# Hybrid decoder trunk: where two retention score stages and two halves of a hidden layer stand in the attention units

## The chip, the cores and the metric

The kernel runs on one core of a Trainium2 chip. The time is that of one execution on the device, in microseconds; the kernel before has a median of 1283.83 us over 3 runs (1283.48 to 1285.69).

## What is computed

Two layers over 256 tokens of width 1024, all in float32. Each layer normalises, projects once into the inputs of three token mixers, joins their outputs and projects back; then comes a channel mixer: a dense SwiGLU in layer 0, a top-2-of-8 expert SwiGLU in layer 1. What the change touches is in the token mixer:

```python
def token_mixer(h, w_in, ...):
    proj = h @ w_in                                # split into q, k_c, v_c, k_s, v_s, k_w, v_w, gates, conv, rq, rk, rv, rg
    o_a = nsa_mixer(...)      # 3 branches: compressed, selected, window (8 heads, 2 kv groups)
    o_b = conformer_conv(...) # GLU, 31-tap depthwise convolution, layer norm, SiLU, 256x256
    o_c = retention(...)      # 4 heads: rotary, (q k^T) * decay, times v, group norm, gate
    return concat[o_a, o_b, o_c] @ w_out

def compress_blocks(kv, pe, w1, w2):               # for keys and for values of the compressed branch
    flat = ...                                     # 15 overlapping blocks of 32 tokens x 64
    return silu(flat @ w1) @ w2                    # w1: 2048 x 256, w2: 256 x 64
```

With 256 tokens every block is selected, so the selected and the window branch are two causal attentions over all keys. Retention in its parallel form is, per head, a masked and decayed 256 x 256 score matrix times the values.

## The kernel before, in words

TensorE does the matmuls (helper `mm`, line 650) and the transposes (helper `flip`, line 653); ScalarE (ACT) does exponentials, SiLUs, table loads and many copies out of PSUM; VectorE (DVE) does maxima, evictions, norms and the convolution's taps. The weights stream through a ring of three slots, loaded by SyncE in the order of `LOADS`; a slot is refilled when its last reader (`LAST_READ`) is through, which for both compression weights is stage `cmpkv`.

The token mixer is one list of stages, `MIXER[l]`, written out by hand: `OPEN`, `HEAD`, twelve attention units, `TAIL`. TensorE, ScalarE and VectorE each walk the same list (function `mixer` in each engine's block) and issue their own part of every stage, in that order. No planner moves anything; an engine that waits holds everything behind it in its queue. Each attention unit k (`UNITS`: branch, kv group, 128 query tokens, heads) contributes, in order:

1. `probT k`: TensorE transposes the probabilities (4 transposes), ScalarE copies them to SBUF (line 1277);
2. what `AHEAD[k]` names (units 6 and 8);
3. `score k+2`: mask matmul and score matmuls; VectorE takes the row maximum (lines 1667, 1669), ScalarE the exponentials (line 1267);
4. what `BESIDE[k]` names: pieces of the other mixers;
5. `pv k`: probabilities times values on TensorE (8 matmuls of 64 columns), VectorE scales and evicts (lines 1674 to 1681).

The stages named in the change and around it:

- `rets k`: retention scores for the keys of half k, four matmuls (8 instructions) into two banks; VectorE multiplies each bank with the decay (line 1740) into `rp0` or `rp1`. `reto` (unit 3) waits for both and multiplies with the values.
- `conv n`: two or so of the 31 taps on VectorE (line 1594); the last ones are in unit 2. `convT` (unit 3) transposes the result on TensorE and waits for the last tap.
- `hid k`: first layer of the compression for keys (k = 0) and values (k = 1), 16 matmuls, 32 instructions `128*32 128x256`, spread over four column groups; ScalarE copies the result (line 1280). `hidT 0` and `hidT 1` use them in unit 6.
- `cnorm 0` and `1`: layer norm of the convolution on VectorE (lines 1771 to 1781), with its root `croot` on ScalarE (lines 1199, 1201). `convB` (unit 6) transposes back; its SiLU (line 1314) brings a table load. `rsilu` and `rroot` bring the second one (line 1259).

PSUM has eight banks. The table `GROUP` gives each stage that writes PSUM the next bank in turn, in the order of the list, `rets` two in a row; `begin` on TensorE waits until the stage that had the bank before has been evicted. So where a stage that takes banks is moved, the stages between its old and its new place get other banks. In the kernel before, `probT 2` takes the bank of `rets 0`, `hid 0` that of `pv 0`, and `hid 1` that of `pv 2`.

Of the kernel before, what the change touches and what calls it, by code (L numbers as in the profile page):

```python
# [76 lines left out]
def conv(a, b):  # L77
    return [("conv", n) for n in range(a, b)]
# [11 lines left out]

AHEAD = {6: [("convB", 0), ("hidT", 0), ("hidT", 1), ("rsilu", 0), ("rroot", 0)], 8: [("retcat", 0)]}

BESIDE = {0: [("rets", 0)] + conv(10, 12), 1: [("rets", 1)] + conv(12, 14), 2: [("hid", 0)] + conv(14, 16),
          3: [("reto", 0), ("convT", 0)], 4: [("cnorm", 0), ("croot", 0), ("hid", 1)],
          5: [("cnorm", 1), ("retnorm", 0)],
          6: [("retnorm", 1)], 7: [("cmpkv", 0), ("conv_pw", 0)],
          8: [("cscore", 0), ("out", 0)], 9: [("out", 1)],
# [7 lines left out]
                           for z in [("probT", k)] + AHEAD.get(k, []) + [("score", k + 2)] * (k + 2 < len(UNITS)) +  # L105
                           BESIDE[k] + [("pv", k)]] + TAIL for l in range(DEPTH)]
EARLIER = (("stat", 0), ("nT", 0), ("stat", 1))
# [2130 lines left out]
```

## Time and profile before

| | |
|---|---|
| median of 3 runs | 1283.83 us (1283.48 to 1285.69) |
| the profiled execution, its own time | 1281.99 us |
| its span (first to last instruction) | 1280.0 us |
| mean granted TensorE clock | 0.997 |
| TensorE, VectorE, ScalarE busy | 98%, 78%, 67% |
| attention units and tail of layer 0 | about 81.5 us to 162 us of the span |
| the same of layer 1 | about 420 us to 504 us |

The span is shorter than the time of its execution by 2.0 us, which lie around it. An engine's busy share is a mean over stages with different limits; the chain of waits, followed back from the last instruction, tells which engine set the end at each point. In a timeline line the number behind the start is the busy time of a group of like instructions, and a bracket gives the idle time before it and who ended it; a group's busy time can overlap the start of the next, because matmuls are pipelined, so distances are read from start to start. The mixer's tiles all lie in one tensor, `arena`, and so the stages are told apart by line and shape: 4 transposes are a `probT` or `convT`, 8 matmuls of 64 columns a `pv`, 32 of `128*32 128x256` a `hid`.

### The profile page before, as it was taken

How to read it: one execution, taken by the hardware profiler on the slowest of the kernel's cores; microseconds unless marked ns; L12 is line 12 of the kernel's file. 1: busy time of each engine (PE TensorE's matmuls, PEld its weight loads, DVE VectorE, ACT ScalarE, POOL GpSimd, SP SyncE). 2: the span in 40 equal slices, each digit the busy share in tenths (PEclk: the TensorE clock that was granted, in tenths of full speed). 3: DMA queues.
4: the chain of work that ended last, by engine and by line, in shares of the span. 5: the costliest groups of instructions: out<-in, count | busy, mean ns of one | idle time of the engine just before them, and what ended most of it. 6: DMA issues, size and time to landing. Idle time of an engine off the chain costs nothing.

```text
span 1280.0 us, 16275 instructions
## 1 busy us (share of the span) xinstructions
PE 1255.0 (98%) x6319; PEld 1016.4 (79%) x6319; DVE 999.7 (78%) x1114; ACT 853.0 (67%) x1219; POOL 31.2 (2%) x21
## 2 busy tenths in 40 slices
PE   9999999999999899999999999999999999999997
PEld 7887578888789776788888888888888888888885
DVE  3698455545448955998899889999889889889897
ACT  3525364444443454878888888878878878878885
POOL 0000000000000000010000000000000000000300
PEclk9999999999999999999999999999999999999999
DMA  9333194552521335899999999999999999999981
GB/s 391 141 143 131 38 372 182 198 197 102 197 99 71 142 132 212 344 401 381 382 371 377 391 373 369 391 381 370 387 377 376 387 371 365 388 375 356 417 365 44
DMA packets 35649, 367.62 MB, mean 287 GB/s; under 512 B 4080, under 2 KB 4208, under 8 KB 8048
## 3 DMA queue, kind: packets, MB, share of 16 engines
q1 hardware_dynamic: 32832, 356.56, 70.6%
q0 software_dynamic: 1440, 5.24, 1.1%
q10 hardware_dynamic: 1296, 4.72, 0.9%
q8 instruction: 53, 0.87, 0.3%
q14 instruction: 28, 0.23, 0.1%
HBM read 360.73 MB, written 5.77 MB: 286 GB/s over the span
## 4 chain that ended last, share of the span: by engine, by line
PE 91%; DVE 6%; ACT 2%; issue 1%; DMA 0%; DVEq 0%; SPq 0%; ACTq 0%
PE ps L650 87%; PE ps L653 4%; DVE arena L1594 1%; DVE wlU L1828 1%; DVE blocks L1649 1%; DMA x<-x_in 0%; DVE arena L1667 0%; DVE wlD L1835 0%; DVE arena L1740 0%; ACT arena L1277 0%; ACT xn L1185 0%; ACT L1259 0%; ACT L1314 0%; DVE xn L2070 0%; ACT whU L1359 0%
## 5 line engine op out<-in xcount | busy, mean ns | idle before, releaser
L1828 DVE TENSOR_TENSOR wlU<-ring,whU 128x2048 fp32r<-128x2048 f32 x198 | 453.4, 2290 | 64.1 <-ACT whU L1359 59.4
L1359 ACT ACTIVATE whU<-ring 128x1024 fp32r<-128x1024 f32 x396 | 417.7, 1061 | 60.7 <-PE ps L650 53.1
L650 PE MATMUL ps<-whU,hTh 128*128 128x512 f32 x880 | 352.9, 401 | 1.7 <-DVE wlU L1828 1.7
L650 PE MATMUL ps<-whU,hTl 128*128 128x512 f32 x880 | 345.0, 392 | 0.0
L650 PE MATMUL ps<-wlU,hTh 128*128 128x512 f32 x880 | 343.0, 390 | 0.0
L1835 DVE TENSOR_TENSOR wlD<-ring,whD 128x2048 fp32r<-128x2048 f32 x97 | 222.1, 2290 | 39.2 <-ACT whD L1371 39.1
L1371 ACT ACTIVATE whD<-ring 128x1024 fp32r<-128x1024 f32 x194 | 205.3, 1067 | 58.9 <-PE ps L650 52.6
L650 PEld LDWEIGHTS ps<-whU,hTl 128*128 128x128 f32 x880 | 165.2, 188 | 36.1
L650 PEld LDWEIGHTS ps<-whU,hTh 128*128 128x128 f32 x880 | 165.3, 188 | 33.8 <-DVE wlU L1828 2.5
L650 PEld LDWEIGHTS ps<-wlU,hTh 128*128 128x128 f32 x880 | 166.1, 189 | 32.4
L650 PE MATMUL ps<-whD,gTh 128*128 128x512 f32 x428 | 168.7, 394 | 0.4 <-DVE gTl L1853 0.4
L650 PE MATMUL ps<-whD,gTl 128*128 128x512 f32 x428 | 167.4, 391 | 0.0
L650 PE MATMUL ps<-wlD,gTh 128*128 128x512 f32 x428 | 166.6, 389 | 0.0
L650 PEld LDWEIGHTS ps<-whD,gTh 128*128 128x128 f32 x428 | 80.4, 188 | 19.6 <-DVE wlD L1835 3.6
L650 PEld LDWEIGHTS ps<-wlD,gTh 128*128 128x128 f32 x428 | 80.8, 189 | 16.5
L650 PEld LDWEIGHTS ps<-whD,gTl 128*128 128x128 f32 x428 | 80.3, 188 | 17.0
L1385 ACT ACTIVATE gTh<-ps 128x256 fp32r<-128x256 f32 x107 | 40.3, 386 | 55.6 <-PE ps L653 55.6
L650 PE MATMUL ps<-arena 128*128 128x64 f32 (+6 forms) x472 | 65.3, 297 | 6.1 <-ACT arena L1277 6.1
L650 PEld LDWEIGHTS ps<-arena 128*128 128x128 f32 (+1 forms) x472 | 56.6, 190 | 18.2 <-issue 16.4
L1628 DVE TENSOR_TENSOR ringl<-ring,whM 128x2048 fp32r<-128x2048 f32 x16 | 36.3, 2288 | 44.1 <-ACT whM L1231 44.1
L1853 DVE TENSOR_TENSOR gTl<-ps,gTh 128x256 fp32r<-128x256 f32 x107 | 44.2, 421 | 28.4 <-ACT gTh L1385 28.4
L653 PE MATMUL ps<-cst,arena 128*128 128x128 f32 x376 | 63.0, 273 | 2.1 <-DVE arena L1594 2.0
(231 smaller groups left out, 1233.3 us busy)
## 6 DMA issues: line engine op xcount, KB each, us to landing
ring<-moe_in SPq DMA_DIRECT2D x88, 2048.0 KB, 8.6
ring<-moe_in SPq DMA_DIRECT2D x88, 1024.0 KB, 8.9
ring<-ffn_in SPq DMA_DIRECT2D x11, 2048.0 KB, 7.6
ring<-mix_in SPq DMA_DIRECT2D x6, 3072.0 KB, 11.7
ring<-ffn_in SPq DMA_DIRECT2D x11, 1024.0 KB, 7.1
ring<-mix_in SPq DMA_DIRECT2D x4, 2048.0 KB, 10.3
ring<-mix_in SPq DMA_DIRECT2D x2, 2176.0 KB, 8.1
ring<-mix_in SPq DMA_DIRECT2D x2, 2112.0 KB, 8.1
```

The costliest lines, as they stand in the source:

```text
L650: return nc.tensor.matmul(o, lhsT, rhs, start=first, stop=last, skip_group_check=True)
L653: return nc.tensor.transpose(o, a, ident)
L1359: A(whU[:, p, :], ring[:, f.slot(J), p * PIECE:(p + 1) * PIECE], ACT.Copy).then_inc(s_hi, 1)
L1371: A(wh_down(f, J, c), ring[:, f.slot(J), (UP + c) * PIECE:(UP + c + 1) * PIECE], ACT.Copy)\
L1385: A(g_high(f, J, i), ps[:, up_bank(f, J, i), 0:FC].rearrange("p (c t) -> p c t", c=DOWN), ACT.Copy)\
L1594: ins = V.scalar_tensor_tensor(out=o, in0=win, scalar=w[:, c, k:k + 1], in1=cacc[:, (CONV_K - k) % 2, c, :], op0=ALU.mult, op1=ALU.add)
L1628: V.tensor_tensor(piece_of(ringl, l, k), piece_of(ring, l, k), whM[k % HOMES][:].bitcast(F32), ALU.subtract).then_inc(s_mlo, 1)
L1649: last = V.tensor_tensor(blocks[lo:lo + HD, v, hi, :, g, 0:NBLK], src[g * HD:(g + 1) * HD, v, :, hi:hi + NBLK, r], spread(pe_[lo:lo + HD, ...
L1828: V.tensor_tensor(wlU[:, w, :], raw, whU[:, w, :].bitcast(F32), ALU.subtract).then_inc(s_lo, 1)
L1835: V.tensor_tensor(wl_down(f, J), raw, high.bitcast(F32), ALU.subtract).then_inc(s_lo, 1)
L1853: V.tensor_tensor(g_low(f, J, i), ps[:, up_bank(f, J, i), 0:FC].rearrange("p (c t) -> p c t", c=DOWN), g_high(f, J, i).bitcast(F32), ALU.s ...
```

## The change

Both `rets` stages stand in unit 1, ahead of its taps; both `hid` stages stand in unit 4, ahead of the convolution's norm and root. Nothing else is edited.

```diff
-BESIDE = {0: [("rets", 0)] + conv(10, 12), 1: [("rets", 1)] + conv(12, 14), 2: [("hid", 0)] + conv(14, 16),
-          3: [("reto", 0), ("convT", 0)], 4: [("cnorm", 0), ("croot", 0), ("hid", 1)],
+BESIDE = {0: conv(10, 12), 1: [("rets", 0), ("rets", 1)] + conv(12, 14), 2: conv(14, 16),
+          3: [("reto", 0), ("convT", 0)], 4: [("hid", 0), ("hid", 1), ("cnorm", 0), ("croot", 0)],
```

The same list feeds both layers and all engines. By the turn of the banks the edit also gives other banks to the stages from `pv 0` to `score 6`: `probT 2` then takes the bank of `pv 0`, `score 3` that of `ks`, `rets 0` those of `kcv` and `score 0`, `hid 0` that of `pv 2` and `hid 1` that of `probT 3`. From `hid 1` on, the banks are those of before.

## Rows read from the trace of the kernel before

**Rows 1.** Busy time by engine, and the chain's shares (page).

```profile
PE 1255.0 (98%) x6319; PEld 1016.4 (79%) x6319; DVE 999.7 (78%) x1114; ACT 853.0 (67%) x1219; POOL 31.2 (2%) x21
...
PE 91%; DVE 6%; ACT 2%; issue 1%; DMA 0%; DVEq 0%; SPq 0%; ACTq 0%
```

**Rows 2.** Busy us by stretch, after its length: PE, PEld, DVE, ACT, POOL; PEclk, DMA share, GB/s.

```profile
81.50:100.60 19.10, 15.74 (x139) 12.83 (x138) 18.49 (x58) 7.24 (x25) 0.00 (x0) 1.00 0.60 238
...
100.60:118.14 17.54, 16.09 (x141) 13.90 (x141) 15.02 (x40) 12.33 (x36) 0.00 (x0) 1.00 0.07 15
...
118.14:170.00 51.86, 51.15 (x233) 32.49 (x234) 25.38 (x61) 21.76 (x50) 0.00 (x0) 1.00 0.44 181
```

**Rows 3.** The chain that ended last, in order of time, layer 0: start, us, what.

```profile
86.19 1.19 DVE arena L1740 x2
...
97.30 3.17 DVE arena L1594 x8
...
118.14 1.08 PE ps L650 x8
```

**Rows 4.** TensorE's timeline, layer 0: start, us, instruction; in brackets idle before, releaser.

```profile
89.03 0.61 PE L653 MATMUL ps<-cst,arena 128*128 128x128 f32 x4
...
91.34 1.93 PE L650 MATMUL ps<-ring,blocks 128*32 128x256 f32 x32 [0.73 <-DVE arena L1681]
94.49 1.08 PE L650 MATMUL ps<-arena 128*128 128x64 f32 x8 [1.22 <-ACT arena L1277]
...
100.60 0.63 PE L653 MATMUL ps<-cst,arena 128*128 128x128 f32 x4 [0.99 <-DVE arena L1594]
...
103.55 1.93 PE L650 MATMUL ps<-ring,blocks 128*32 128x256 f32 x32
105.41 1.10 PE L650 MATMUL ps<-arena 128*128 128x64 f32 x8
106.35 0.61 PE L653 MATMUL ps<-cst,arena 128*128 128x128 f32 x4
...
106.90 1.03 PE L650 MATMUL ps<-arena 128*128 128x256 f32 x4
109.10 1.08 PE L650 MATMUL ps<-arena 128*128 128x64 f32 x8 [1.17 <-ACT arena L1277]
```

**Rows 5.** VectorE's timeline, layer 0.

```profile
90.86 0.42 DVE L1681 TENSOR_TENSOR arena<-ps,arena 128x256 f32<-128x256 f32 x1
91.20 0.68 DVE L1667 TENSOR_REDUCE arena<-ps 128x4 f32<-128x512 f32 x1
...
108.22 0.68 DVE L1667 TENSOR_REDUCE arena<-ps 128x2 f32<-128x512 f32 x1
```

**Rows 6.** ScalarE's timeline, layer 0.

```profile
101.88 0.47 ACT L1267 ACTIVATE arena<-ps,arena 128x256 f32<-128x256 f32 x1 [2.53 <-DVE arena L1669]
...
103.08 0.60 ACT L1277 ACTIVATE arena<-ps 128x512 f32<-128x512 f32 x1 [0.17 <-ACT arena L1267]
...
109.14 0.47 ACT L1267 ACTIVATE arena<-ps,arena 128x256 f32<-128x256 f32 x1 [0.18 <-DVE arena L1669]
...
110.72 0.60 ACT L1277 ACTIVATE arena<-ps 128x512 f32<-128x512 f32 x1 [0.56 <-PE ps L653]
111.33 1.28 ACT L1314 ACT_TABLE_LOAD   x1
```

**Rows 7.** TensorE's timeline, layer 1, at pv 5.

```profile
447.90 1.07 PE L650 MATMUL ps<-arena 128*128 128x64 f32 x8 [1.17 <-ACT arena L1277]
```

**Rows 8.** TensorE's timeline, layer 1, the router's matmuls.

```profile
500.30 3.64 PE L650 MATMUL ps<-router,hTr 128*128 128x8 f32 x32
```

**Rows 9.** Busy time by stretch of 1 us behind the router's matmuls (the last columns: clock, DMA).

```profile
504.00:505.00 1.00, 1.00 (x11) 0.90 (x9) 0.93 (x7) 0.00 (x0) 0.00 (x0) 0.94 1.16 483
505.00:506.00 1.00, 0.93 (x5) 0.32 (x3) 0.92 (x5) 0.00 (x0) 0.00 (x0) 0.50 0.84 360
...
508.00:509.00 1.00, 1.00 (x8) 0.86 (x7) 1.00 (x2) 0.41 (x1) 0.00 (x0) 0.85 0.78 328
```

## The prediction, written before the changed kernel was run

> **What bounds the kernel now.** I read the page's busy shares and its chain of waits first [rows 1]. TensorE is busy 98% of the span, the chain stays on it for 91% and leaves it for VectorE for 6%. A stage moved inside a stretch that TensorE owns costs nothing and gains nothing; what counts is the few places where the chain is elsewhere. So the second view is the busy time by stretch, cut at the attention units [rows 2]. From 81.50 to 100.60 us (units 0 to 3 of layer 0) VectorE is busy 18.49 of 19.10 us and TensorE 15.74: VectorE sets the pace. From 100.60 to 118.14 us TensorE has 16.09 of 17.54 us, VectorE 15.02, ScalarE 12.33: a stretch passed from hand to hand. From 118.14 us on TensorE is full (51.15 of 51.86 us), so whatever delay stands there is carried to the end of the layer. The chain in order of time says the same: the depthwise convolution's taps on VectorE up to 100.47 us, and from 118.14 us TensorE [rows 3]. Last come the three engines' own timelines, where each stage can be found by its shape [rows 4 to 6]: what TensorE waits for in units 2 to 5, and how VectorE and ScalarE queue. Layer 1 has the same pattern, 338.80 us later [rows 7]; what is worked out for layer 0 counts twice.
>
> **Retention scores: unit 0 to unit 1.** TensorE's work (score stage 0, 8 matmuls) and VectorE's (two multiplies, 1.19 us of the chain at 86.19 us [rows 3]) keep their size. On VectorE, unit 0's taps begin 1.19 us earlier, so the eviction of pv 0 goes from 90.86 to 89.67 us and the row maximum of score 3 from 91.20 to 90.01 us [rows 5]; then the two retention stages come together and the taps of unit 1 start where they started. VectorE had no idle time there, has the same instructions, and ends the taps at 100.47 us as before [rows 3]. I cost this part at nothing; VectorE's queue hides it.
>
> The rotation of banks adds one wait: the transposes of probabilities 2 now take the bank of pv 0, which VectorE frees at 89.67 + 0.42 = 90.09 us, about 1 us after TensorE started them before (89.03 us [rows 4]). Behind them wait score 4, whose maximum VectorE takes only after all taps of unit 1, and ScalarE's copy, itself behind the exponentials of score 3, which move 1.19 us earlier with their maximum. If that cover were gone, it would be 1.06 us (90.09 against 89.03 us), in the stretch where TensorE has 3.36 us of room [rows 2].
>
> **First half of the compression's hidden layer out of unit 2.** It is 32 matmuls in 1.93 us, at 91.34 us, and it waited 0.73 us for pv 0's eviction [rows 4]. Removing it empties TensorE, but what TensorE does next waits for others: pv 2 waited 1.22 us for ScalarE, and the convolution's transposes at 100.60 us waited 0.99 us for the last tap on VectorE [rows 4]. The tap is still done at 100.47 us. So the gain is nothing: TensorE arrives some 1.2 us earlier and idles some 2.2 us instead of 0.99 before 100.60 us. The copy on ScalarE moves too; before, ScalarE stood idle 2.53 us after it [rows 6], so its removal gains nothing either.
>
> **The same half into unit 4.** Here TensorE is not waiting. The second half runs from 103.55 to the start of pv 4 at 105.41 us, 1.86 us [rows 4]; two halves back to back end at 103.55 + 2 x 1.86 = 107.27 us. The banks they want (pv 2's and probabilities 3's) come free before the convolution's transposes are through, by the order of the stages, and the weights are in: the second half's did not wait at 103.55 us, and the first half's load stands ahead of them in the queue. Then, by starts of before:
> - pv 4 takes 106.35 - 105.41 = 0.94 us, probabilities 5 with the mask of score 7 106.90 - 106.35 = 0.55, score 7 itself 1.03 [rows 4]. Score 7 is full at 107.27 + 0.94 + 0.55 + 1.03 = 109.79 us, against 107.93.
> - VectorE took its maximum at 108.22 us; it stood behind the convolution norm and pv 4, so 108.22 - 107.93 = 0.29 us had passed since score 7 was full. Now it starts as soon as the matmul is done, with 0.03 us for the hand-over, at 109.82 us, 1.60 later. Behind it wait cnorm 1, retnorm 0 and all of unit 5 on VectorE.
> - The exponentials of score 7 began 109.14 - 108.22 = 0.92 us after the maximum [rows 5, 6]: now 110.74 us. From the first exponential of such a unit to the next copy are 103.08 - 101.88 = 1.20 us [rows 6]: the copy of probabilities 6 comes at 111.94 us instead of 110.72. It had waited 0.56 us for TensorE, which is why only 1.22 us of the 1.60 arrive.
> - TensorE's side is earlier than that: transposes 5 are full near 108.8, their copy near 109.4, pv 5 follows score 7 at once, and transposes 6 are full near 111.2. The convolution's back-transposes wait for cnorm 1, which follows the maximum of score 7 on VectorE, until about 111.3 (all four worked out with the same spacings).
> - From the copy on, ScalarE is a chain without a gap: table load at 111.33 us directly behind it [rows 6], SiLUs, second table load, root, exponentials 8, copy 7, and then pv 7 on TensorE at 118.14 us [rows 3]. All of it shifts by 1.22 us; TensorE's own work ahead of pv 7 is late by less than that and adds nothing.
>
> ScalarE's two small copies now stand ahead of the convolution's root; the second half is full at about 107.3 us, and cnorm 0 on VectorE gives the root its input only shortly before the maximum of score 7 could start at 108.22 us, so they fit. SyncE's load of the second output weights waits for the compression's last matmul; that moves by no more than 1.22 us, and what reads these weights moves as far.
>
> The bounds per layer: below, 1.86 - 1.17 = 0.69 us, if the idle 1.17 us ahead of pv 5 [rows 4] swallows its part and the exponentials of score 7 don't hold up the copy; above, 1.86 us, if no idle time absorbs anything. I take 1.22, from the row of a copy behind exponentials, which is the order in which ScalarE's queue is written.
>
> For the length of the added stage the Trainium skill would say otherwise: "TensorE: Matmul & The Clock Gate", section "Back-to-back issue gap", gives N/2.4 + 2.5 ns for an isolated matmul, that is 109 ns for 256 columns and 3.5 us for 32 of them. The trace disagrees: 1.86 us for 32 [rows 4], four column groups of 32 side by side. By the page the sum would be about 1.6 us more per layer.
>
> **Sum.** 2 x 1.22 = 2.44 us. The profiled execution has a span of 1280.0 us and a time of 1281.99 us; with the change 1282.4 and 1284.4. The median of the runs is 1283.83 us, 1.84 above the profiled one; the forecast for the median is 1283.83 + 2.44 = 1286.3 us, 0.19% slower.
>
> **Rivals.**
> A. *The clock falls in the emptied stretch.* In layer 1 TensorE did router matmuls of 8 columns from 500.30 us [rows 8], and then the granted clock is 0.50 in the row at 505 us (and in the two after it), the lower level of 1.2 GHz; with the parts in the rows at 504 and 508 us, 0.12 and 0.30 us, it is low for 3.4 us [rows 9]. In units 0 to 3 it never fell (granted 1.00 [rows 2]), though TensorE idled 0.73, 1.22 and 0.99 us. The change takes 1.93 us of dense matmuls out of there and makes one gap some 2.2 us. If the clock fell near 101 us and stayed low as long as in that place, 3.4 x 0.5 = 1.7 us of TensorE's would be lost in just the stretch where it now is on the path. Once: 2.44 + 1.7 = 4.1, 1288.0 us; in both layers 5.8, 1289.7 us. For it: the gap, and the 64-column matmuls before it. Against: in that other place the low clock followed 3.5 us of matmuls that hardly use the array, much longer than this gap.
> The Trainium skill's page "TensorE: Matmul & The Clock Gate", section "HAM oscillation — how this bites in real kernels", describes kernels in which TensorE falls back to the lower clock because it waits between bursts, each time anew; that is this rival.
>
> B. *Not slower: units 0 to 3 get shorter.* The maximum of score 3 comes 1.19 us earlier, and with it exponentials, copies and pv 2. If the stretch to 100.60 us were ended by that chain and not by the taps, each layer would gain up to 1.19 us there and pay 0.69 to 1.22 behind it: -0.50 to +0.03 us per layer, 1282.8 to 1283.9 us; I put it at 1283.4. For it: TensorE's waits at 91.34 and 94.49 us are for VectorE and ScalarE. Against: the last wait before 100.60 us is for the tap, with VectorE busy 97%. It decides only if VectorE's taps themselves end earlier than 100.47 us.
>
> C. *Only the floor.* The exponentials of score 7 turn out to be covered: 2 x 0.69 = 1.4, 1285.2 us. Against: they are ahead of the copy in ScalarE's queue, and they can't begin before score 7 is full.
>
> **How the numbers follow.** A 0.18, B 0.09, C 0.15, the forecast 0.58. 0.2% is 2.57 us (about what a measurement of this kernel tells from no change), so the forecast, at 2.44, is at the border itself. Slower by over 0.2%: A whole, and of the forecast a good half, 0.31: 0.49. Within: the rest of the forecast 0.27, C, and B but for 0.07 of it: 0.44. Faster 0.07. The range takes in C, half of B and A in one layer: 1283.7 to 1288.3 us.
>
> **What would show it.** Right: the last tap ends at about 100.47 us, as now; TensorE's idle time before the convolution's transposes over 2 us; two groups of 32 matmuls in a row from there + 3 us; the maximum of score 7 1.6 us later and pv 7 1.2 us later, relative to the last tap; no further difference to the end of the layer. Wrong: a granted clock under 1.00 near 102 us (A); a last tap that ends earlier (B); copy 6 waiting for TensorE and not for ScalarE's exponentials (C); or a difference that grows in the feed-forward passes, where I expect none.

## The result, and the profile after

The changed kernel takes 1288.52 us (median of 7 runs, 1286.41 to 1290.14) against 1283.83 us: 4.7 us slower, ratio 1.0038 with a 95% interval of 1.0028 to 1.0047. Its profiled execution took 1290.14 us, span 1288.1: it is the slowest of the seven. Medians and intervals here leave out three executions far above all others, one of the kernel before (3588.64 us) and two of experiments (1678.39 and 1580.37 us). The forecast was 1286.3 us and the range ended at 1288.3, 0.2 us short.

The page of the changed kernel: busy time by engine, granted clock in 40 slices, the chain's shares.

```profile
PE 1261.2 (98%) x6319; PEld 1022.2 (79%) x6319; DVE 1000.3 (78%) x1114; ACT 853.3 (66%) x1219; POOL 31.3 (2%) x21
...
PEclk9998999999999999999999999999999999999999
...
PE 91%; DVE 5%; ACT 2%; issue 1%; DMA 0%; DVEq 0%; SPq 0%; ACTq 0%
```

The counts are those of [rows 1]; TensorE is 6 us busier with the same 6319 matmuls. The slice with an 8 is the fourth, from about 97 to 129 us: units 3 and on of layer 0. The stretches of [rows 2], changed kernel:

```profile
81.50:100.60 19.10, 15.13 (x106) 12.99 (x106) 18.62 (x58) 6.86 (x24) 0.00 (x0) 0.90 0.60 238
100.60:118.14 17.54, 17.25 (x148) 14.02 (x149) 12.02 (x31) 9.16 (x29) 0.00 (x0) 0.82 0.00 1
118.14:170.00 51.86, 50.83 (x240) 32.34 (x240) 28.11 (x68) 21.47 (x50) 0.00 (x0) 1.00 0.39 152
```

The granted clock, the third number from the end, was 1.00 in all three before; now it is 0.90 and 0.82 in the first two. In the second TensorE is busy nearly throughout, and VectorE and ScalarE get less done. Where it is low, in stretches cut near the falls (a stretch of which a part lies outside shows a little over 0.50, the level of 1.2 GHz), and once more in layer 1 and behind the router:

```profile
90.30:93.70 3.40, 3.29 (x14) 2.36 (x12) 3.37 (x10) 2.10 (x9) 0.00 (x0) 0.56 0.97 403
93.70:100.50 6.80, 4.69 (x40) 4.46 (x40) 6.66 (x21) 1.62 (x5) 0.00 (x0) 0.97 0.05 20
100.50:107.30 6.80, 6.80 (x41) 5.86 (x45) 3.59 (x11) 1.82 (x6) 0.00 (x0) 0.52 0.00 0
...
445.30:448.70 3.40, 3.40 (x27) 2.58 (x29) 1.64 (x6) 1.03 (x3) 0.00 (x0) 0.56 0.00 0
...
510.10:516.90 6.80, 6.80 (x38) 5.38 (x39) 5.02 (x22) 1.50 (x2) 0.00 (x0) 0.52 1.01 428
```

TensorE's timeline of layer 0, answering [rows 4]: transposes 2, score 4, the convolution's transposes, both halves, pv 4, and pv 7.

```profile
90.00 1.12 PE L653 MATMUL ps<-cst,arena 128*128 128x128 f32 x4 [0.95 <-DVE arena L1681]
...
100.46 1.09 PE L653 MATMUL ps<-cst,arena 128*128 128x128 f32 x4 [2.11 <-DVE arena L1594]
...
106.06 4.08 PE L650 MATMUL ps<-ring,blocks 128*32 128x256 f32 x64
110.08 1.10 PE L650 MATMUL ps<-arena 128*128 128x64 f32 x8
...
122.19 1.08 PE L650 MATMUL ps<-arena 128*128 128x64 f32 x8 [0.33 <-ACT arena L1277]
```

The foreseen waits are there: 0.95 us for pv 0's bank, 2.11 us for the last tap. What was not in the forecast is the pace behind them: from 100.46 us to the first half takes 5.60 us, where [rows 4] have 2.95, and the same four transposes show 1.09 us instead of 0.63. VectorE waits for it (maxima of score 6 and 7), and ScalarE's copy 6 and table load follow, answering [rows 5, 6]:

```profile
81.61 3.50 DVE L1649 TENSOR_TENSOR blocks<-ps,par 64x120 f32<-64x120 f32 x16 [1.08 <-PE ps L650]
...
106.17 0.69 DVE L1667 TENSOR_REDUCE arena<-ps 128x4 f32<-128x512 f32 x1 [2.49 <-PE ps L650]
...
112.64 0.69 DVE L1667 TENSOR_REDUCE arena<-ps 128x2 f32<-128x512 f32 x1 [1.06 <-PE ps L650]
```

```profile
113.57 0.47 ACT L1267 ACTIVATE arena<-ps,arena 128x256 f32<-128x256 f32 x1 [1.25 <-DVE arena L1669]
...
114.76 0.60 ACT L1277 ACTIVATE arena<-ps 128x512 f32<-128x512 f32 x1 [0.17 <-ACT arena L1267]
115.38 1.28 ACT L1314 ACT_TABLE_LOAD   x1
```

Copy 6 now waits for the exponentials of score 7 on its own engine (0.17 us), and no longer 0.56 us for TensorE: the queue works as forecast. Layer 1, where the clock falls at 444.9 us, 1.5 us behind the end of the gap of 2.18 us, and the transposes right after the gap still run at full pace:

```profile
443.42 0.63 PE L653 MATMUL ps<-cst,arena 128*128 128x128 f32 x4 [2.18 <-DVE arena L1594]
...
447.69 3.94 PE L650 MATMUL ps<-ring,blocks 128*32 128x256 f32 x64
...
463.67 1.08 PE L650 MATMUL ps<-arena 128*128 128x64 f32 x8 [0.32 <-ACT arena L1277]
```

A yardstick for all that follows is the distance from VectorE's first eviction of the compression input (line 1649, or 1654 in kernels with five lines added above it) to pv 7: it leaves out what lies before and behind. Before it is 36.37 us in layer 0 (81.77 to 118.14) and the same in layer 1. After it is 122.19 - 81.61 = 40.58 and 463.67 - 424.58 = 39.09 us: 4.2 and 2.7 us more. The two profiled executions differ by 8.1 us of span; 6.9 are these, and 1.3 lie behind the router's matmuls, where the clock is low for 6.8 us instead of 3.4 [rows 9]. The profiles of the kernels below have 0, 3.4 or 6.8 us there.

Each execution is told with its mean clock, and twice its missing part times the span is the time at the low level, wherever it lies (an estimate, good to about 1.3 us, since the clock has three digits). For the kernel before, 98 executions beside the experiments: 2.6 to 20.6 us at the low level, 12.5 in the mean, and their time rises by 0.33 us with each us of it (correlation 0.92). For the changed kernel 18.0 to 25.7, mean 21.7. So the kernel before seems to lose to the clock as well, and the execution that I had read, with 7.7 us, was one of those that lose least.

### The profile page after: what moved, and what is told of

The parts are those of the page before. It is cut to its first block, busy times and chain, and to the rows that moved or that the text cites. A ratio compares the mean times of both kernels' runs of the same rounds, so it can differ in the third digit from the quotient of the medians.

```text
span 1288.1 us, 16275 instructions
## 1 busy us (share of the span) xinstructions
PE 1261.2 (98%) x6319; PEld 1022.2 (79%) x6319; DVE 1000.3 (78%) x1114; ACT 853.3 (66%) x1219; POOL 31.3 (2%) x21
## 4 chain that ended last, share of the span: by engine, by line
PE 91%; DVE 5%; ACT 2%; issue 1%; DMA 0%; DVEq 0%; SPq 0%; ACTq 0%
PE ps L650 88%; PE ps L653 4%; DVE arena L1594 1%; DVE wlU L1828 1%; DVE blocks L1649 1%; DMA x<-x_in 0%; DVE arena L1667 0%; DVE wlD L1835 0%; ACT arena L1267 0%; DVE arena L1740 0%; ACT xn L1185 0%; ACT L1259 0%; ACT L1314 0%; ACT arena L1277 0%; DVE xn L2070 0%
## 5 line engine op out<-in xcount | busy, mean ns | idle before, releaser
L650 PEld LDWEIGHTS ps<-arena 128*128 128x128 f32 (+1 forms) x472 | 60.1, 199 | 15.8 <-issue 9.0
L650 PE MATMUL ps<-arena 128*128 128x64 f32 (+6 forms) x472 | 68.1, 305 | 4.0 <-ACT arena L1277 3.7
L653 PEld LDWEIGHTS ps<-cst,arena 128*128 128x128 f32 x376 | 49.2, 146 | 22.8 <-issue 7.6
```

Source lines behind the costliest of these rows:

```text
L650: return nc.tensor.matmul(o, lhsT, rhs, start=first, stop=last, skip_group_check=True)
L653: return nc.tensor.transpose(o, a, ident)
```

## The experiments

Two theories stood. *Clock and queue*: a moved half costs about 1.2 us per layer through ScalarE's queue, and the emptied units 1 to 3 let TensorE's clock fall, which costs the rest. Against it, in turn: the new bank wait, the added work alone, or that the low clock only marks idle time. All runs stand beside the kernel before, in three groups, where its median was 1283.79, 1284.02 and 1284.42 us; ratios are to the kernel before of the same group.

**Only the retention scores moved.**

```diff
-BESIDE = {0: [("rets", 0)] + conv(10, 12), 1: [("rets", 1)] + conv(12, 14),
+BESIDE = {0: conv(10, 12), 1: [("rets", 0), ("rets", 1)] + conv(12, 14),
```

> Only the retention scores moved (both in unit 1); both halves of the hidden layer stay where they were. Theory 'clock and queue' (the whole cost comes from the moved half: 1.2 us per layer through ScalarE's queue in unit 4, and the rest because TensorE's emptied units 1 to 3 let its clock fall): no difference, 1.000 of the time before within 0.1%, granted clock 1.00 in units 0 to 5 of both layers. Rival 'bank' (the new wait of transposes 2 for pv 0's eviction is what empties TensorE and costs): 1 to 2 us slower, with a clock under 1.00 behind that wait.

1283.38 us, ratio 0.9999 (0.9990 to 1.0008): no difference, as expected. The expected clock of 1.00 was wrong. TensorE of this kernel, transposes 2 to first half, with the clock low from 90.9 us:

```profile
90.37 0.66 PE L653 MATMUL ps<-cst,arena 128*128 128x128 f32 x4 [0.95 <-DVE arena L1681]
90.86 0.39 PE L650 MATMUL ps<-causalb,identb 128*128 128x256 bf16 x1
91.04 1.91 PE L650 MATMUL ps<-arena 128*128 128x256 f32 x4
92.88 2.60 PE L650 MATMUL ps<-ring,blocks 128*32 128x256 f32 x32
...
100.83 0.63 PE L653 MATMUL ps<-cst,arena 128*128 128x128 f32 x4 [0.27 <-DVE arena L1594]
```

Score 4 takes 1.91 us instead of 1.03, and yet pv 7 comes at 36.36 us from the first eviction: the wait for the last tap (0.27 us left of 0.99) takes it all up. In layer 1 the clock fell for 3.4 us too, in the same place, and the distance is 36.38 us. So the rival was right that the new wait for a bank (0.95 us) can be followed by a fall, and wrong that it costs: these falls, in units 1 and 2, were free.

**Only the first half moved.**

```diff
-          2: [("hid", 0)] + conv(14, 16), ... 4: [("cnorm", 0), ("croot", 0), ("hid", 1)],
+          2: conv(14, 16), ...            4: [("hid", 0), ("hid", 1), ("cnorm", 0), ("croot", 0)],
```

> Only the first half of the hidden layer moved from unit 2 to unit 4 (both halves together ahead of the convolution's norm); the retention scores stay apart. 'Clock and queue': all of the loss, 4 to 5 us slower (0.3 to 0.4%), clock falls in units 2 to 5 in at least one layer of the profiled execution, pv 7 later than the last tap by 1.2 us more than before where the clock did not fall, and by 2.5 to 4 us where it did. 'Bank': 2.4 us slower or less, no fall.

1286.29 us, ratio 1.0022 (1.0010 to 1.0033): some 2.5 to 2.8 us, a good half of the loss, less than I expected. Time at the low level is 19.5 us in the mean of its executions. In the profiled one TensorE idles 3.88 us ahead of pv 2; from about there the clock is low for 3.4 us in layer 0 and 6.8 in layer 1, and the distances are 37.95 and 38.74 us:

```profile
94.30 1.30 PE L650 MATMUL ps<-arena 128*128 128x64 f32 x8 [3.88 <-ACT arena L1277]
```

The queue's share alone would be 2.3 us of the 2.5 to 2.8 (below), which leaves next to nothing for 6.9 us more at the low level; the slope of 0.33 would ask for 2.3. Its interval overlaps that of the full change. Why the falls cost so little at the median here, and what the retention scores add when both are moved, is not settled.

**The changed kernel, kept busy in its gaps.** And the kernel before likewise. `keep_busy(o, n)` issues n bf16 matmuls of zeros, 256 columns; the kernel before has this helper already and uses it in other places, as at its start and behind the router's matmuls.

```diff
 # stage convT, changed kernel: 18, kernel before: 8
                         o = begin(l, stage)
+                        keep_busy(o, 18)
                         pe.wait_ge(s_conv, l + 1)
 # stage pv, changed: 12, before: 10
                         o = begin(l, stage, k)
+                        if k == 2:
+                            keep_busy(o, 12)
 # stage probT, changed kernel only
+                        if k == 2:
+                            keep_busy(begin(l, "score", 4), 8)
 # stage hid, kernel before only
+                        if k == 0:
+                            keep_busy(begin(l, "pv", 2), 6)
```

> The changed kernel with small bf16 matmuls of zeros added on TensorE in its three gaps of units 2 and 3 in both layers (8 ahead of transposes 2, 12 ahead of pv 2, 18 ahead of the convolution's transposes, each into a bank that the next stage overwrites); they fit into the idle time. 'Clock and queue': the granted clock stays 1.00 in the units, and what is left is the queue's share: 2.4 us slower than before (1.2 per layer), that is about 2.3 us faster than the changed kernel. Rival 'no clock' (the low clock only shows idle time and costs nothing, the loss is another wait): as slow as the changed kernel, 4.7 us.

> The kernel before with such matmuls in its own gaps (6 ahead of the first half of the hidden layer, 10 ahead of pv 2, 8 ahead of the convolution's transposes). 'Clock and queue': the kernel before is granted the full clock in its units in nearly all executions, so no difference (within 0.1%). If some of its executions (1281.6 to 1285.7 us) pay for a fallen clock there, up to 1 us faster. Rival 'added matmuls cost by themselves': 1 us or more slower, and the run of the changed kernel with them has to be read with that.

The changed kernel goes to 1285.35 us, ratio 1.0009 (1.0000 to 1.0017); the kernel before to 1281.76, ratio 0.9987 (0.9978 to 0.9996). Both gain, 3.2 and 2.0 us by the medians, 3.7 and 1.7 by the ratios, with nothing but dummy work added. TensorE's stretches of the changed kernel with it, layer 0 and 1: the clock is 1.00.

```profile
81.50:100.60 19.10, 17.47 (x144) 15.38 (x143) 18.33 (x57) 7.08 (x26) 0.00 (x0) 1.00 0.60 238
100.60:119.50 18.90, 18.30 (x177) 15.11 (x175) 15.21 (x42) 12.93 (x37) 0.00 (x0) 1.00 0.09 16
...
440.60:459.50 18.90, 18.30 (x177) 15.11 (x175) 15.21 (x42) 12.93 (x37) 0.00 (x0) 1.00 0.08 17
```

And its layer 1, first eviction and pv 7:

```profile
421.92 3.50 DVE L1654 TENSOR_TENSOR blocks<-ps,par 64x120 f32<-64x120 f32 x16 [1.26 <-PE ps L650]
```

```profile
459.46 1.08 PE L650 MATMUL ps<-arena 128*128 128x64 f32 x8 [0.32 <-ACT arena L1282]
```

The distance is 37.54 us, in layer 0 too: 1.17 us over 36.37. That is the queue's share by itself, and the forecast had 1.22. Up to 0.1 us of it may be the dummy work's own: with 18 of them TensorE has no idle time left, and the transposes start 0.24 us after the last tap, not 0.15 as in the changed kernel. Between the two kernels with dummy work lie 1285.35 - 1281.76 = 3.6 us by the medians, 3.2 by the means and 2.8 by the ratios; two queue shares (2.3) and 2.2 us more at the low level account for most of it. I had not expected the kernel before to gain. Its executions of 1284 us and more spend 15.1 us at the low level in the mean, the others 9.5; in which stage they do is not recorded, since only one execution of each kernel is profiled.

**The gap without the added work.** In both kernels 12 of the 16 matmuls of the first half are left out, so they compute less than the task asks and serve to measure time alone.

```diff
-                        for j in range(16):
+                        for j in range(16 if k else 4):
-                                      w[:, j, :], j < 4, j >= 12)
+                                      w[:, j, :], j < 4, j >= 12 or not k)
```

> The kernel before, with 24 of the 32 instructions of the first half of the hidden layer left out in unit 2 (12 of its 16 matmuls; the keys' compression is then incomplete): units 2 and 3 are emptied as by the change, and nothing is added in unit 4. Queue's share: 0 us, pv 7 at the same distance from the first compression eviction (36.4 us) in a layer where the clock stays up. Clock: it falls in units 2 to 4 in most executions; a fall that reaches unit 4 or 5 costs 0.3 to 1.5 us. Together 0.5 to 1.5 us slower than before. Rival 'it is only the added work in unit 4': no difference.

> The changed kernel with the same 12 matmuls left out where they now stand, in unit 4. The queue's share should be gone (0.46 us of matmuls remain against 0.29 us of cover and 0.56 us of slack before copy 6), the emptied gaps stay: 'clock and queue' expects 1.5 to 2.5 us slower than before, that is about 2.3 us faster than the changed kernel, with falls of the clock as there. Rival 'it is only the added work': as fast as before.

The emptied kernel before has less to do and takes longer: 1286.11 us, ratio 1.0015 (1.0003 to 1.0028), some 2 us and more than the 0.5 to 1.5 that I expected. Its layer 1 in the profiled execution:

```profile
420.00:430.00 10.00, 9.53 (x77) 8.27 (x77) 8.47 (x29) 4.51 (x18) 0.00 (x0) 1.00 0.72 278
434.60:448.30 13.70, 13.66 (x61) 13.12 (x62) 8.65 (x26) 3.44 (x11) 0.00 (x0) 0.50 0.01 4
448.30:463.00 14.70, 13.54 (x123) 11.69 (x121) 11.93 (x29) 10.31 (x32) 0.00 (x0) 1.00 0.10 17
```

That is 13.7 us at the low level, through units 2 to 4, from the end of a gap of 2.52 us ahead of pv 2 on, and a distance of 463.62 - 421.92 = 41.70 us; in layer 0, 6.8 us and 37.98. This execution is the slowest of its eleven. The emptied changed kernel takes 1286.87 us by the median; its ratio, 1.0009 (0.9996 to 1.0022), does not tell it from no change, nor from the 1.5 us that I expected at least. It is faster than the changed kernel by 1.7 us (medians) to 3.7 (ratios). In its profiled execution the falls are as expected, 10.2 us in the units of each layer, and the distances are 39.32 and 39.12 us.

**The same with dummy work in the gaps** (6, 22 and 8 ahead of the first half, pv 2 and the convolution's transposes in the kernel before; 8, 12 and 18 in the changed one).

> The emptied kernel before (24 of the 32 instructions of the first half of the hidden layer left out in unit 2) with small bf16 matmuls of zeros in the gaps: 6 ahead of that half, 22 ahead of pv 2, 8 ahead of the convolution's transposes. 'Clock': what the emptied kernel loses comes back in full, 1281.8 us, as the kernel before with such matmuls (2 us faster than before), low clock only behind the router and at the end. Rival (the emptied kernel loses by something else): slower than before by 1.5 us, as without them.

> The changed kernel with the same 24 instructions left out in unit 4, and the small matmuls of the changed kernel's version in its gaps (8, 12 and 18). 'Queue': without the 1.4 us of matmuls in unit 4 the distance from the first compression eviction to pv 7 is 36.4 to 36.6 us instead of 37.54, in both layers, and the time 1281.8 to 1282.3 us, 3 us less than with the whole half. Rival (the unit's order or the other banks cost, not the matmuls): 37.5 us and 1285 us stay.

1281.97 us, ratio 0.9985 (0.9976 to 0.9994), distance 36.32 us in both layers: what the emptied kernel lost is back. And the changed kernel without the 24 instructions: 1282.72 us, ratio 0.9985 (0.9976 to 0.9994), with a distance a little under the 36.4 us expected. Its first eviction, the remaining 40 instructions, pv 7:

```profile
81.62 3.49 DVE L1654 TENSOR_TENSOR blocks<-ps,par 64x120 f32<-64x120 f32 x16 [1.08 <-PE ps L650]
```

```profile
103.47 2.37 PE L650 MATMUL ps<-ring,blocks 128*32 128x256 f32 x40
...
117.87 1.08 PE L650 MATMUL ps<-arena 128*128 128x64 f32 x8 [0.33 <-ACT arena L1282]
```

36.25 us against 37.54 with all 64. So the queue's share is due to the added matmuls; the other banks and the new order cost nothing that shows in the distance.

**Both halves in unit 2**, where TensorE waits.

```diff
-          2: [("hid", 0)] + conv(14, 16), ... 4: [("cnorm", 0), ("croot", 0), ("hid", 1)],
+          2: [("hid", 0), ("hid", 1)] + conv(14, 16), ... 4: [("cnorm", 0), ("croot", 0)],
```

> Both halves of the hidden layer in unit 2, retention scores as before: TensorE's work is brought into the gap and not out of it. It should be through in time for the last tap (about 100.2 us against 100.6), so nothing is added; copy 5 on ScalarE follows the root without a copy between them, 0.27 us earlier per layer. 'Clock and queue': 0.5 us faster where the clock stays up, but TensorE now idles some 2.9 us ahead of pv 5, so the clock may fall there; the next stages are waited for by ScalarE, which would take the gain back: between 0.5 us faster and 1.5 us slower. Rival 'no clock': 0.5 us faster, steadily.

> The same with small bf16 matmuls of zeros in its gaps: 6 ahead of the first half, 3 ahead of the convolution's transposes, 24 ahead of pv 5. 'Clock and queue': the clock stays up in the units, 2.5 us faster than before, and 0.5 us faster than the kernel before with such matmuls. Rival: no better than that one.

> Both halves in unit 2 with small matmuls in the gaps (6 ahead of the first half, now into the bank of the second half, which is free; 3 ahead of the convolution's transposes, 24 ahead of pv 5). The earlier version waited 3.12 us for a bank. Expected: 36.1 to 36.2 us from first compression eviction to pv 7 in both layers, 1281.3 us, 2.5 us faster than the kernel before.

Without dummy work: 1285.85 us, ratio 1.0017 (1.0005 to 1.0028), some 2 us slower where I expected 1.5 at most. Layer 0 of the profiled execution gains the 0.27 us (distance 36.10); in layer 1 the clock is low from 448.4 to 455.2 us, behind the gap ahead of pv 5, now 2.51 us for 1.17 before, and the distance is 38.95 us:

```profile
447.12 1.08 PE L650 MATMUL ps<-arena 128*128 128x64 f32 x8 [2.51 <-ACT arena L1277]
448.03 1.56 PE L653 MATMUL ps<-cst,arena 128*128 128x128 f32 x8
449.39 1.75 PE L650 MATMUL ps<-fold,arena 128*128 128x32 f32 x8
```

The first version with dummy work was a mistake of mine: 1289.29 us, ratio 1.0038 (1.0025 to 1.0051). Its matmuls asked for the bank of pv 2, which in this order is that of score 3 and held until its exponentials are done:

```profile
93.45 0.83 PE L650 MATMUL ps<-warm 128*128 128x256 bf16 x6 [3.12 <-ACTq L1277]
```

With the right bank: 1281.55 us, ratio 0.9986 (0.9977 to 0.9995), distance 35.98 us in both layers. Of the kernels that compute everything it is the fastest, level with the kernel before plus dummy work (1281.76, distance 36.32); the 0.34 us per layer between their traces is beyond what the runs can tell.

**More dummy work** (10 more ahead of pv 5 in the kernel before).

> The kernel before with small matmuls as in its first version (6, 10, 8) and 10 more ahead of pv 5. 'Clock': no execution falls in the units, so those of 1283 us and more of the first version are gone: median 1281.6 us, highest under 1283. Rival (falls come from elsewhere): the same spread as the first version.

1282.63 us, ratio 0.9989 (0.9980 to 0.9998), 1281.18 to 1284.18: no better than the first version (1281.37 to 1283.58), so the rival held. The profiled execution is at the low level only behind the router and at the end, and where the slower executions lose their time is open.

## Why the prediction failed

- *Retention scores*: right. VectorE ends its taps 18.7 us after the first eviction in each profiled kernel, and moving them alone changes nothing.
- *First half out of unit 2*: this is the step that failed. "The gain is nothing" is right, and so is "idles some 2.2 us instead of 0.99" (measured 2.11 and 2.18), but the cost of that idle time was put at nothing too. At the end of it or shortly behind it the clock fell, in both layers of the profiled execution, and the stages on the path ran at about half pace: 5.60 us for 2.95 in layer 0.
- *First half into unit 4*: right, 1.17 us per layer (1.1 without the dummy work's part) for 1.22. The two halves take 3.59 us, not 3.72, and copy 6 waits where it was said to wait.
- *The price of the Trainium skill's page for the half* ("TensorE: Matmul & The Clock Gate", section "Back-to-back issue gap", 1.6 us more per layer): not borne out, 3.59 us for 64 instructions where 109 ns each would be 7.0.
- *Sum*: so it has a term for the queue, 2.44 us, and none for the clock. "In units 0 to 3 it never fell" was read from one execution, and that one (1281.99 us) was among the fastest. I put the 1.84 us between it and the median aside as a constant; by the slope above, the 4.8 us that it spent less at the low level (7.7 against 12.5) are worth 1.6 of them. Measured are 4.7 us, of which 2 x 1.17 = 2.3 are queue. The other 2.4 go with 9.2 us more at the low level (21.7 against 12.5), 0.26 us for each, beside 0.33 in the kernel before. The dummy work gives a check: it gains more in the changed kernel than in the kernel before, by 1.1 us (medians) to 2.0 (ratios). So between 1.1 and 2.4 us of the change's cost are the clock's, and up to 1.3 us stay unassigned.
- *Rival A*, given 0.18, is what happened, in both layers of the profiled execution. Its place and mechanism hold, and so does its price, half of the time at the low level on the path: in layer 0 the clock stayed low for 6.8 us across the last tap and cost 4.21 - 1.17 = 3.0 us, in layer 1 for 3.4 us and 1.5. That its 1288.0 us for one layer is so near the measured 1288.52 is luck: the clock fell in both, and an execution of median time must have lost less than the profiled one.
  The argument against it, that the low clock had followed something much longer, was wrong. In the changed kernel it fell with no gap of more than 2.2 us near it: in layer 0 once within the wait of 0.95 us for the bank and once at the end of the 2.11 us, in layer 1 behind the 2.18. Nor was the place behind the router empty before its fall: from 503.79 us 14 dummy matmuls of 256 columns ran there, and the clock fell about 1.1 us into them.
  The Trainium skill's page "TensorE: Matmul & The Clock Gate", section "HAM oscillation — how this bites in real kernels", describes the same pattern, short bursts with waits between them and a low clock at each burst. The trace agrees as to the pattern, with 0.56 and 0.52 granted in the stretches above; the waits of the page's kernel are longer, about 3 to 5 us for 0.95 to 2.2 here.
- *Rivals B and C* fall: the last tap did not move, and copy 6 waited for ScalarE.

## What to carry to other kernels

TensorE's idle time next to the critical path is not free: work moved out of a gap leaves the gap wider, and where the clock then fell, what came after the gap ran at about half pace (5.60 us for 2.95). It cost only where it reached into stages on the path. Before a stage is moved, look at the mean clock of several executions, not at one profile; a spread of 0.3% with one kernel was the first sign here. Cheap matmuls that fill the waits, 24 per layer, gained the kernel before 2 us (0.13%); 18 of them take 1.96 us, and they must go into a bank that is free by then, or they wait for it (3.12 us in one experiment).

## What the runs showed of the hardware

- Leaving out 24 matmul instructions per layer made the kernel slower by 0.15%, and filling the gaps with matmuls of zeros then made it faster than the kernel before by 0.15%.
- Time against time at the low level, in 98 executions of one kernel: 0.33 us per us, correlation 0.92.
- A fall can come behind the gap: in layer 1 of the changed kernel the gap of 2.18 us ended at 443.42 us, TensorE was busy from then on, and the clock fell at 444.9.
- A fall was free where TensorE waited anyway: with the retention scores moved alone it was low for 3.4 us in each layer, at no cost.
- The low clock slowed transposes of 128 columns (4 in 1.09 us for 0.63) and matmuls of 256 (4 in 1.91 for 1.03) alike.
